# Turning layer 0's attention weights by DMA transposes instead of TensorE transposes, in a two-layer encoder trunk on one core

## The reference, cut to what matters

```python
h = x @ w_in                      # q, k, v of both groups, and forget gates
# stick-breaking heads (s < t):
z = (q @ k.T) * dh**-0.5
log_stay = where(mask, log_sigmoid(-z), 0)
after = cumsum(log_stay, reverse=True) - log_stay
w = where(mask, exp(log_sigmoid(z) + after), 0);   out = w @ v
# forgetting heads (s <= t):
logits = (q @ k.T) * dh**-0.5 + cum[t] - cum[s]
p = softmax(where(mask, logits, -inf));            out = p @ v
# then concat(outs) @ w_o, LayerNorm, conv FFN, LayerNorm; and layer 1, a sparse attention, likewise
```

## Time and profile before

| what | value |
|---|---|
| median of 3 runs | 2886.86 us (2885.72 to 2887.35) |
| profiled execution, first to last instruction | 2882.5 us |
| median less span (what lies around it) | 4.4 us |
| TensorE busy | 2773.1 us, 96% |
| VectorE busy | 1876.8 us, 65% |
| GpSimd busy | 1653.8 us, 57% |
| ScalarE busy | 1081.0 us, 38% |
| mean granted TensorE clock | 0.995 of full |
| DMA moved in the whole span | 240.57 MB |

### The profile page before, as it was taken

How to read it: one execution, slowest core, us unless ns; L and a number is a source line. 1 busy time by engine, 2 the same in 40 slices (tenths; PEclk the granted TensorE clock), 3 DMA queues, 4 the chain that set the end, 5 groups by cost and what they waited for, 6 DMA issues and landing times.

```text
span 2882.5 us, 44624 instructions
## 1 busy us (share of the span) xinstructions
PE 2773.1 (96%) x16630; PEld 1456.3 (51%) x16912; DVE 1876.8 (65%) x2733; ACT 1081.0 (38%) x1765; POOL 1653.8 (57%) x918
## 2 busy tenths in 40 slices
PE   8999998899999999998899999999999999999998
PEld 4566665454444444444444444677764444444443
DVE  6777666486666674256999999677756756665042
ACT  4556555343333310014554333666653433332000
POOL 4777545336666669845347777600003566665884
PEclk9999999999999999999999999999999999999999
DMA  4222222431111143222113222211113211113322
GB/s 147 60 59 63 71 56 48 161 118 59 59 59 59 66 171 129 102 73 79 52 37 146 102 93 82 74 59 44 58 63 120 88 52 59 59 59 117 135 101 101
DMA packets 102990, 240.57 MB, mean 83 GB/s; under 512 B 42448, under 2 KB 42576, under 8 KB 102848
## 3 DMA queue, kind: packets, MB, share of 16 engines
q1 hardware_dynamic: 56352, 204.13, 19.9%
q10 hardware_dynamic: 46496, 34.48, 4.6%
HBM read 185.31 MB, written 31.51 MB: 75 GB/s over the span
## 4 chain that ended last, share of the span: by engine, by line
PE 85%; DVE 4%; ACT 3%; issue 3%; POOL 2%; ACTq 1%; DMA 0%; POOLq 0%; DVEq 0%
PE ps L1503 23%; PE ps L317 20%; PE ps L306 13%; PE ps L2310 6%; PE ps L584 5%; PE ps L341 3%; PE ps L2346 2%; PE ps L590 2%; PE ps L694 2%; PE ps L1830 2%; PE ps L779 2%; PE ps L756 2%; PE ps L2325 1%; PE ps L1874 1%; DVE pt_lo L715 1%
## 5 line engine op out<-in xcount | busy, mean ns | idle before, releaser
L262 POOL TENSOR_TENSOR w_hi<-w_stage,ones 128x1024 bf16<-128x1024 f32 (+1 forms) x115 | 235.1, 2044 | 137.9 <-PE ps L317 85.2
L265 POOL TENSOR_TENSOR w_lo<-w_stage,w_hi 128x1024 bf16<-128x1024 f32 (+1 forms) x115 | 262.6, 2283 | 9.0
L1320 DVE SCALAR_TENSOR_TENSOR x_res<-x_res,ps 128x1024 f32<-128x1024 f32 x32 | 39.0, 1218 | 338.1 <-PE ps L317 337.2
L317 PE MATMUL ps<-w_hi,hid_hi 128*128 128x512 bf16 x689 | 206.2, 379 | 1.6 <-POOL w_lo L265 0.8
L317 PE MATMUL ps<-w_lo,hid_hi 128*128 128x512 bf16 x690 | 206.4, 379 | 0.7
L317 PE MATMUL ps<-w_hi,hid_lo 128*128 128x512 bf16 x690 | 206.3, 379 | 0.7
L2310 PE MATMUL ps<-lat_hi,q_now 128*128 128x512 bf16 (+3 forms) x730 | 185.9, 323 | 1.2
L306 PE MATMUL ps<-xt_hi,w_hi 128*128 128x512 bf16 x598 | 179.2, 380 | 3.1 <-DVE score L1989 2.5
L306 PE MATMUL ps<-xt_hi,w_lo 128*128 128x512 bf16 x596 | 178.6, 380 | 0.8 <-issue 0.2
L306 PE MATMUL ps<-xt_lo,w_hi 128*128 128x512 bf16 x592 | 178.2, 381 | 0.8
L1503 PE MATMUL ps<-xt_lo,w_hi 128*128 128x512 bf16 x426 | 161.5, 379 | 0.5
(11 more groups left out here) (295 smaller groups left out, 7873.1 us busy)
## 6 DMA issues: line engine op xcount, KB each, us to landing
w_stage<-in_l_up SPq DMA_DIRECT2D x88, 512.0 KB, 3.2
w_stage<-in_l_down SPq DMA_DIRECT2D x88, 512.0 KB, 3.2
w_stage<-in_l_o SPq DMA_DIRECT2D x32, 512.0 KB, 4.7
w_stage<-in_l_q SPq DMA_DIRECT2D x32, 512.0 KB, 5.2
q_split<-q_out SPq DMA_DIRECT2D x32, 512.0 KB, 2.6
q_now<-q_split SPq DMA_DIRECT2D x16, 1024.0 KB, 4.8
w_stage<-in_l_qkv SPq DMA_DIRECT2D x24, 512.0 KB, 3.3
x_spilled<-x_res ACTq DMA_DIRECT2D x16, 512.0 KB, 2.6
```

Of the source, the lines that this page charges most:

```text
L262: pool.tensor_tensor(w_hi[slot][:, 0:cols], w_stage[slot][:, 0:cols], ones[:, 0:1].to_broadcast([P, cols]), ALU.mult).then_inc(w_cast[slot ...
L265: pool.tensor_tensor(w_lo[slot][:, 0:cols], w_stage[slot][:, 0:cols], w_hi[slot][:, 0:cols], ALU.subtract).then_inc(w_split[slot], 1)
L317: mm = pe.matmul(ps[:, bank + h, :], a[:, k, rows], w[slot][:, h * HALF:(h + 1) * HALF], start=(k == 0 and m == 0), stop=(k == tiles - 1 a ...
```

## The change

The weights are split before they are turned. POOL now writes the weights to `take` in both kinds of head. ACT writes their high part and DVE their low part, both from and to SBUF in one instruction a step, into a buffer `split` that holds, for each block of 128 keys, 128 columns of high and 128 of low. One DMA transpose a step, issued by SP, turns all blocks of both parts into `turned`; the product with v reads from there. ACT and DVE do this in slot t + 3 (`HI_AFTER = 0`). `split[b]` lies in the same bytes as `prob[b]`, so the scan and the exponential of step t now wait for the DMA transpose of step t - 4 to have landed. A step's transpose moves between 2 and 16 blocks of 128 x 128 bf16 (64 KB to 512 KB), and there are 128 of them. SP's list is written out, with the loads of weights at fixed places between transposes. The memsets of `prob`'s edge column go; the sb product covers n - 1 columns. PSUM banks 5 and 6 are no longer used in this stage.

```diff
+HI_AFTER = 0
...
+            pair = sb(f"split{b}", [P, TB, 2, P], BF16, place.at)
+            return place(f"prob{b}", [P, SEQ], F32), pair
...
-        pt_hi = [room("pt_hi0", [P, TB, 512], BF16), room("pt_hi1", [P, TB // 2, 512], BF16)]
-        pt_lo = [room("pt_lo0", [P, TB, 512], BF16), room("pt_lo1", [P, TB // 2, 512], BF16)]
+        turned = [room("turned0", [P, TB, 2, 512], BF16), room("turned1", [P, TB // 2, 2, 512], BF16)]
...
-        class Turning:
...
+        def weights_hi(act, kind, pair, t):
+            src, hi, _ = split_views(t)
+            if kind == "sb":
+                act.wait_ge(s_wsb, STEPS * pair + t + 1)
+            else:
+                act.wait_ge(s_wfox, STEPS * (pair - N_SB // 2) + t + 1)
+            act.activation(hi, src, ACT.Copy).then_inc(s_whi, 1)
+
+        def weights_lo(dve, pair, t):
+            src, hi, lo = split_views(t)
+            dve.wait_ge(s_whi, STEPS * pair + t + 1)
+            dve.tensor_tensor(lo, src, hi, ALU.subtract).then_inc(s_wlo0, 1)
+
+        def weights_turn(sp, pair, t):
+
+            m, g, qs = query_block(t) + 1, t % 8 // 4, query_block(t) % 4 * P
+            sp.wait_ge(s_wlo0, STEPS * pair + t + 1)
+            if t % 4 == 0:
+                wait_if(sp, s_pv, 4 * pair + t // 4 - 1)
+            sp.dma_start_transpose(turned[g][:, 0:m, :, qs:qs + P].rearrange("p j a n -> p (j a) n"),
+                                   split[t % 4][:, 0:m, :, :].rearrange("p j a n -> p (j a n)")
+                                   ).then_inc(s_turn[t % 4], 16)
...
-                        pe.wait_ge(turning.lo, BATCHES * p + batches_through(4 * group + 3))
+                        for b in range(4):
+                            pe.wait_ge(s_turn[b], turned_through(p, 4 * group + b))
...
-                if kind_then == "sb":
-                    turning.turn(pe, p, t, s_wsb, STEPS * p + t + 1)
-                elif kind_then == "fox":
-                    turning.turn(pe, p, t, s_wfox, STEPS * (p - N_SB // 2) + t + 1)
...
-                    act.wait_ge(turning.made, turning.prob_free(pair, t))
+                    act.wait_ge(s_turn[t % 4], turned_through(pair, t) - 16)
...
-                    wait_if(dve, turning.made, turning.prob_free(p1, t1))
+                    wait_if(dve, s_turn[t1 % 4], turned_through(p1, t1) - 16)
...
-                pool.tensor_tensor(prob[t % 4][:, 0:n], take[t % 4][:, 0:n], prob[t % 4][:, 0:n],
+                pool.tensor_tensor(take[t % 4][:, 0:n - 1], take[t % 4][:, 0:n - 1], prob[t % 4][:, 0:n - 1],
...
-            load_rest(sp, feed_qkv)
-            load_first(sp, feed_o0)
+            for n, pair in ((0, 1), (1, 1), (2, 1), (0, 2), (1, 2)):
+                load_piece(sp, feed_qkv, n, pair)
+            ahead = {4: (2, 2), 8: (0, 3), 13: (1, 3)}
+            for pair in range(N_PAIRS):
+                for t in range(STEPS):
+                    weights_turn(sp, pair, t)
+                    n, further = ahead.get(t, (0, N_PAIRS))
+                    if pair + further < N_PAIRS:
+                        load_piece(sp, feed_qkv, n, pair + further)
```

More of the change, by code:

```diff
@@ L524, in program, with weight_buffer @@
         stay = [low(f"stay{b}", [P, SEQ], F32) for b in range(2)]
-        prob = [low(f"prob{b}", [P, SEQ], F32) for b in range(2)]
+        def weight_buffer(place, b):
+            pair = sb(f"split{b}", [P, TB, 2, P], BF16, place.at)
+            return place(f"prob{b}", [P, SEQ], F32), pair
+        weights = [weight_buffer(low, b) for b in range(2)]
         assert low.at <= arena
@@ L529, in program @@
         mix_lo = room("mix_lo", [P, KT, SEQ], BF16)
-        prob += [room(f"prob{b}", [P, SEQ], F32) for b in range(2, 4)]
+        weights += [weight_buffer(room, b) for b in range(2, 4)]
+        prob, split = [w[0] for w in weights], [w[1] for w in weights]
         take += [room(f"take{b}", [P, SEQ], F32) for b in range(2, 4)]
@@ L723, in program, with turned_through, split_views @@
-        turning = Turning("att0", prob, pt_hi, pt_lo, s_pv)
+        def turned_through(pair, t):
+            return 16 * (4 * pair + t // 4 + 1)
+        def split_views(t):
+            n = (query_block(t) + 1) * P
+            pair = split[t % 4][:, 0:query_block(t) + 1, :, :]
+            return take[t % 4][:, 0:n].rearrange("p (j n) -> p j n", n=P), pair[:, :, 0, :], pair[:, :, 1, :]
+        def weights_hi(act, kind, pair, t):
[5 more added lines that the diff above has]
+            act.activation(hi, src, ACT.Copy).then_inc(s_whi, 1)
@@ L771, in pair_tensor @@
                     if part == 0:
-                        pe.wait_ge(turning.lo, BATCHES * p + batches_through(4 * group + 3))
+                        if prev is None and group == 0:
+                            pe.wait_ge(s_pjl, 6)
+                        for b in range(4):
+                            pe.wait_ge(s_turn[b], turned_through(p, 4 * group + b))
                         wait_if(pe, s_ol, 4 * p + group)
@@ L992, in heads_sync @@
         def heads_sync(sp):
-            load_rest(sp, feed_qkv)
-            load_first(sp, feed_o0)
+            for n, pair in ((0, 1), (1, 1), (2, 1), (0, 2), (1, 2)):
[7 more added lines that the diff above has]
+                        load_piece(sp, feed_qkv, n, pair + further)
+                    if (pair, t) == (N_PAIRS - 2, 8):
+                        load_piece(sp, feed_o0, 2, 0)
+                if pair == N_PAIRS - 3:
+                    for n in (3, 0, 1):
+                        load_piece(sp, feed_o0, n, 0)
         def heads_gpsimd(pool):
@@ L999, in heads_gpsimd @@
                 split_qkv_lo(pool, n, 1)
-            pool.wait_ge(s_edge, 4)
             with pool.Fori(0, N_SB // 2) as pair:
@@ L1057, in heads_vector @@
                 proj_evac_lo(dve, e, 0)
-            for b in range(4):
-                dve.memset(prob[b][:, P - 1:SEQ:P], 0.0).then_inc(s_edge, 1)
-            dve.wait_ge(s_edge, 4)
             all_pairs(dve, pair_vector)
```

30 lines of the change are left out of this document (15 added, 15 removed).

## The result

| | before | after |
|---|---|---|
| median of the runs (range, count) | 2886.29 us (2884.92 to 2887.35, 4) | 2942.88 us (2939.68 to 2944.61, 4) |
| span of the profiled execution | 2882.5 us | 2942.4 us |
| ratio (95% interval) | 1 | 1.0190 (1.0176 to 1.0205) |

What follows compares the result with a forecast made beforehand. TensorE, 96% busy, was taken to bound most of the heads stage; removing its transposes, less landing waits, gave -20 - 19 + 7 = -32 us: 2855 us against 2886.86, own range 2830 to 2878, wide range 2818 to 2990.

Steps and rivals of the forecast that it cites:

- The sum: Heads stage: four sb pairs -20 us, three fox pairs -19, last pair and tail +7, net -32 us.
- What bounds the kernel now: Heads stage: TensorE holds 55.8 us of work a pair; nearly all of a fox pair's chain, 36 of 60 us in sb.
- the loop of landings: Fox pairs: exponential of step t waits for the transpose of t - 4; steps 4 to 7 need 15.2 us, not 12.
- What replaces the splits: Sb pairs: SBUF low parts cost 10.9 to 14.9 us against some 12.3; pairs come to 55 to 56 us.
- rival 4: Sb pairs: DVE slower beside POOL, 3.14 us instead of 1.2 a full low part; no gain, 2875 us; inside forecast's range.
- What the transpose costs: DMA transposes in the heads stage: 1.6 us fixed plus 0.41 a key block, 29 us of queue per pair.
- Rival 3: Heads stage: the transpose queue (DMA engines or SP's issue) becomes the bound; slower, 2893 to 2990 us or beyond; chance 0.38.
- Where the landing is waited for: Fox exponentials wait for the transpose of four steps before, 2.5 us lost a half; a fox pair takes 53 us.
- The last pair: Last pair, not bound by TensorE: landing loop adds 3.2 us in each half and 1 at the tail.
- The 4.4 us around the span: Whole kernel: 4.4 us added to the predicted span of 2850.5 us to give the measured time of 2855 us.
- rival 2: Fox and last pairs: a full step lands after 8 us, fox pairs about 61 us; 2890 us, no change; chance 0.07.

Runs made afterwards that it cites:

- e6: Changed kernel with own split buffers for fox pairs and DVE's low part reading stale PSUM banks (output not the reference's): 2884.04 us, ratio 0.9990 to before.
- e9: Kernel before with three needless matmuls ahead of each accumulation of the projections, 4.0 us more TensorE work per pair: 2903.03 us, ratio 1.0048.
- e5: Kernel before with 192 TensorE transposes instead of 576 and nothing in their place (output not the reference's): 2887.23 us, ratio 1.0002.
- e10: e5 with 24 needless matmuls of 128 columns (1.4 us) in slot 12 of each pair: 2882.77 us, ratio 0.9979 to the kernel before.
- e14: Kernel before with the copies of q and k issued from SyncE instead of ScalarE in the fox pairs: 2882.59 us, ratio 0.9978.
- e15: Sb pairs as before; fox by DMA transpose, own buffers, later v product, SyncE copies; pairs 6, 7 project into two banks; needless matmuls in last pair: 2878.52 us.
- e2: Changed kernel with DVE's low part reading its f32 operand from stale PSUM banks instead of SBUF: 2901.56 us, ratio 1.0047 to before.
- e3: Changed kernel with the fox pairs' split in four buffers of its own, so only the high part waits for the landing: 2918.03 us, ratio 1.0109 to before.
- e11: Sb pairs as before, fox by DMA transpose with own buffers and later v product, plus needless matmuls in fox slots 11, 12 and the last pair: 2884.55 us.
- e1: Changed kernel with each DMA transpose replaced by a plain copy of the same bytes (weights not turned): 2933.25 us, ratio 1.0159 to before.

## Why the prediction was wrong, point by point

- *The sum*: it had -20 us for the sb pairs, -19 for the three fox pairs and +7 for the last. Measured are +32.8, +18.8 and +11.5. e6, which takes both new costs away, gives 59 us back and ends level with before, so the gain of the forecast isn't there either. Two steps failed: what the freed time of TensorE is worth, and what the low part costs from SBUF.
- *What bounds the kernel now*: half right. Work added to TensorE did lengthen a pair (e9). The step that failed is the one from there to "what it gives up is gained". It credited 5 us in an sb pair, and in a fox pair the whole way from 59.3 us down to TensorE's 47.9, of which the loop of landings took 5 back. 5.3 us less of it gave 0 (e5), and e6, with 7.9 us less and both new costs gone, gave 0.1%. One reason is the granted clock, which fell to 0.94 in both; with it full, 3.9 us less gave 2.1 us in a fox pair (e10). Other bounds of a fox pair stand close behind TensorE: ACT's seven issues (e14) and the one projection bank (e15, where pairs reach the forecast's 53 us). In an sb pair they are read from the chain and not tested: in e6, between 117 and 238 us, DVE's scans are 13.5% of it, ACT's issuing 10.5% and the landing of the copies of q and k 9.5%. No rival on the list had any of these, though in the earlier trace rows the first part of each half ran through DVE.
- *What replaces the splits*: this term was mis-sized, and with it the sign. 12.5 us of low parts per sb pair became 21.3 (three pairs, 37.4 to 64.0 us), beyond the 10.9 to 14.9 that I had allowed. I scaled the row by columns. The added cost isn't one of columns: a low part of any size that comes behind POOL's instruction waits for its end. The 3.14 us at its upper end was the sign, and I gave it to rival 4 with the price "no gain". The scans were held up too (27.2 to 30.0 us a pair), and so were POOL's own instructions (42.4 to 46.8). Forecast 5 us less a pair, measured 8.2 more. e2 gives nearly all of it back.
- *What the transpose costs*: right. 4.2 us for a full step (forecast 4.85, bounds 3.1 to 4.9), the queue 45.5% in use. Rival 3, slower by the queue, was false, though the outcome lay in its band of times: a right sign for a wrong reason.
- *Where the landing is waited for*: the place was right (exponentials of the fox steps), the size wrong. 65.9 us, not 53. The low part in the loop took up to 2.50 us instead of 1.2 to 1.7, landings beside ACT's copies 7.0 to 8.2 us, and the waits held 35 steps, not the four large ones of a half alone. e3 gives 25 us back, in the fox pairs and the last.
- *The last pair*: +11.5 us, forecast +7. The sum took only the landings into account. Up to its last `mix_hi` the pair lasts 52.8 us before and 64.3 after, 59.9 without the wait for landings (e3), 61.1 without DVE's second SBUF operand (e2) and 54.9 with neither (e6). So 3.2 to 5.0 us of it was the low part again.
- *The 4.4 us around the span*: 1.8 us in the run of after (2944.19 less 2942.4). The rest of the 4.4 is that the profiled execution of before was quicker than the median.
- *Rival 4* named the mechanism of the sb pairs, *rival 2* that of the fox pairs (its 61 us was short of 65.9). Each had its place; the mistake was to price them one at a time, and both below what they cost. That the two together would outweigh the gain was in no case.

What isn't settled: how much of the lost gain is the clock. In the fox pairs full clock goes with pairs 1.5 to 2.8 us shorter than e5's. In the last pair it costs nothing (e11). In the sb pairs no run with fewer transposes kept the full clock, so it is open there.

## What to carry to other kernels

That an engine is 96% busy doesn't say that work taken off it is gained: before crediting it, take a part of that work away and nothing else, and see whether the time moves, and the clock with it. When an operand moves from PSUM to SBUF, look at what POOL does at that moment: what a DVE instruction with two SBUF operands pays on top of its own time is the rest of POOL's instruction, whatever its own size. Work moved off an engine frees other things too: here the engine time alone gave nothing (e5), and a second PSUM bank on top of it made two pairs 5 us shorter each (e15).

## What the runs showed of the hardware

- A DVE instruction of 128 columns with two SBUF operands took 2.09 us beside a POOL product, and 0.28 us with one operand in PSUM.
- An SBUF-to-SBUF DMA transpose of 512 KB landed in 4.2 us, a copy of the same bytes in 4.1 (e1's undisturbed full step). The transposes took SP 1.17 to 4.7 us each to issue, median 1.30, the copies in their place 0.59 (e1), the copies of q and k on ACT mostly 0.5 to 0.6.
- With less work on TensorE its granted clock was lower, 0.94 for 1.00 over 240 us (e5), and one gap of 2.7 us was followed by matmuls at 1.2 GHz.
